# The split weight tiles of gate and up, moved from 224 to 64 bytes off the 2 KB raster

## The reference

```python
def swiglu(h, w_gate, w_up, w_down):
    return (jax.nn.silu(h @ w_gate) * (h @ w_up)) @ w_down

h = rms_norm(x, g_ffn1_pre)
x = x + 0.5 * rms_norm(swiglu(h, w_ffn1_gate, w_ffn1_up, w_ffn1_down), g_ffn1_post)
h = rms_norm(x, g_mix_pre)
# token mixing: one projection of h, stick-breaking attention (8 heads x 64),
# retention (4 heads x 128), two gated branches, one output projection
x = x + rms_norm(merged @ w_out, g_mix_post)
h = rms_norm(x, g_ffn2_pre)
x = x + 0.5 * rms_norm(swiglu(h, w_ffn2_gate, w_ffn2_up, w_ffn2_down), g_ffn2_post)
```

## Time and profile before

| | us |
|---|---|
| median of 3 runs | 1366.22 |
| lowest and highest | 1366.1 and 1368.4 |
| the profiled execution | 1366.35 |
| its span | 1364.3 |
| TensorE busy | 1349.2 |
| VectorE busy | 1029.3 |
| ScalarE busy | 734.3 |

### The profile page before, as it was taken

How to read it: one execution, slowest core, us unless ns; L and a number is a source line. 1 busy time by engine, 2 the same in 40 slices (tenths; PEclk the granted TensorE clock), 3 DMA queues, 4 the chain that set the end, 5 groups by cost and what they waited for, 6 DMA issues and landing times.

```text
span 1364.3 us, 22732 instructions
## 1 busy us (share of the span) xinstructions
PE 1349.2 (99%) x8668; PEld 1209.1 (89%) x8668; DVE 1029.3 (75%) x1124; ACT 734.3 (54%) x1008; POOL 99.9 (7%) x156
## 2 busy tenths in 40 slices
PE   8999999999999999999999999999999999999998
PEld 7999999999888888777778888799999999988886
DVE  7987888788988964667664334689788878888896
ACT  6554554555765743666653233555454455458663
POOL 0000000001330000322210000000000000025000
PEclk9999999999999999999999999999999999999999
DMA  6333332347994555212113345333333234399844
GB/s 209 109 92 109 123 108 82 117 123 248 197 202 155 191 179 139 77 48 63 47 47 93 93 122 189 106 100 113 113 123 108 80 120 123 112 284 198 177 139 154
DMA packets 152935, 177.71 MB, mean 130 GB/s; under 512 B 5552, under 2 KB 116400, under 8 KB 152752
## 3 DMA queue, kind: packets, MB, share of 16 engines
q1 hardware_dynamic: 139536, 151.54, 35.2%
q0 software_dynamic: 13056, 25.17, 10.2%
q10 hardware_dynamic: 288, 0.26, 0.1%
HBM read 170.66 MB, written 6.29 MB: 130 GB/s over the span
## 4 chain that ended last, share of the span: by engine, by line
PE 91%; DVE 4%; ACT 2%; DMA 1%; issue 1%; POOL 0%; SPq 0%; DVEq 0%; ACTq 0%; POOLq 0%
PE ps L797 14%; PE ps L800 14%; PE ps L799 14%; PE ps L898 8%; PE ps L899 7%; PE ps L900 7%; PE ps L730 6%; PE ps L732 5%; PE ps L731 5%; PE ps L737 2%; PE ps L738 2%; PE ps L739 2%; PE ps L1090 1%; DMA w_raw<-w_ffn_up 1%; PE ps L1045 1%
## 5 line engine op out<-in xcount | busy, mean ns | idle before, releaser
L797 PE MATMUL ps<-s_hi,u_hi 128*128 128x256 f32 x960 | 268.0, 279 | 1.5 <-DVE u_lo L1805 0.8
L800 PE MATMUL ps<-s_hi,u_lo 128*128 128x256 f32 x960 | 267.7, 279 | 0.0
L799 PE MATMUL ps<-s_lo,u_hi 128*128 128x256 f32 x960 | 267.7, 279 | 0.0
L797 PE MATMUL ps<-a_hi,u_hi 128*128 128x256 f32 x808 | 225.7, 279 | 1.1 <-DVE a_lo L1760 1.1
L800 PE MATMUL ps<-a_hi,u_lo 128*128 128x256 f32 x808 | 225.4, 279 | 0.0
L799 PE MATMUL ps<-a_lo,u_hi 128*128 128x256 f32 x808 | 225.3, 279 | 0.0
L1291 ACT ACTIVATE u_hi<-w_sum 128x1024 fp32r<-128x1024 f32 x120 | 124.0, 1057 | 173.0 <-DVE w_sum L1834 80.3
L797 PEld LDWEIGHTS ps<-s_hi,u_hi 128*128 128x128 f32 x960 | 180.5, 188 | 2.1 <-ACT m_c L1325 1.1
L799 PEld LDWEIGHTS ps<-s_lo,u_hi 128*128 128x128 f32 x960 | 180.5, 188 | 0.0
L800 PEld LDWEIGHTS ps<-s_hi,u_lo 128*128 128x128 f32 x960 | 180.5, 188 | 0.0
L898 PE MATMUL ps<-w_hi,l_hi 128*128 128x512 f32 x448 | 174.9, 390 | 0.1
(11 more groups left out here) (222 smaller groups left out, 2529.1 us busy)
## 6 DMA issues: line engine op xcount, KB each, us to landing
w_raw<-w_ffn_gate SPq DMA_DIRECT2D x64, 512.0 KB, 5.2
w_raw<-w_ffn_up SPq DMA_DIRECT2D x64, 512.0 KB, 4.7
d_sum<-w_ffn_down POOLq DMA_DIRECT2D x48, 512.0 KB, 12.3
w_raw<-w_in SPq DMA_DIRECT2D x44, 512.0 KB, 4.2
w_raw<-w_ffn_down SPq DMA_DIRECT2D x40, 512.0 KB, 4.2
d_sum<-w_ffn_down SPq DMA_DIRECT2D x16, 512.0 KB, 8.0
x_tok<-x SPq DMA_DIRECT2D x8, 512.0 KB, 6.0
d_m_raw<-w_ffn_down SPq DMA_DIRECT2D x8, 512.0 KB, 8.4
```

Of the source, the lines that this page charges most:

```text
L797: pe.matmul(o, wh, hi[:, k, :], start=first and f == 0 and k == 0, stop=False, skip_group_check=True)
L799: pe.matmul(o, wh, lo[:, k, :], start=False, stop=False, skip_group_check=True)
L800: mm = pe.matmul(o, wl, hi[:, k, :], start=False, stop=last and k == KH - 1, skip_group_check=True)
```

## The change

One constant is changed. It moves the start of `u_hi`, `u_lo` and `w_sum` in all seven slots.

```diff
 LINE = 2048
 GAP = 512
-UP_OFF = 224
+UP_OFF = 64
```

## The result

The kernel after takes 1361.26 us, median of 14 runs, against 1366.34 of before; the ratio is 0.9927 with an interval of 0.991 to 0.9945. It is faster, where 1384 was forecast, and inside the range given (1348 to 1387). The single runs say more than the median. Before: eight between 1365.8 and 1366.4 us, six between 1368.4 and 1368.9. After: five at 1351, seven at 1361 and two at 1371 us, and nothing between.

What follows compares the result with a forecast made beforehand. The prediction took TensorE's matmul start-to-start distance to bound the kernel. 1366.3 us plus 17.7 us (3.33 ns on 5304 matmuls with u) gave 1384.0 us, range 1348 to 1387.

Steps and rivals of the forecast that it cites:

- TensorE alone bounds the loops; an edit of its distance is paid in full.: Gate-and-up loops of both FFNs: time is the number of matmuls times the start-to-start distance, 116.7 ns, with TensorE never waiting.
- VectorE, ScalarE and the queues cost nothing.: Subtractions and copies into the moved tiles: offsets 0 and 224 within 2 ns, priced at nothing; no DMA changed.
- The distance with u at 224 is 116.7, with b22 on the grid 120.0, and the place of the stationary tile is the difference.: Gate-and-up matmuls: 3.3 ns longer with the stationary tile on the streamed tile's 512-byte grid than 224 off it.
- The rule of the Trainium skill: Weight loads on TensorE: separate read ports, so no offset matters and the time is 1366 us; basis of the no-change rival, 0.28.
- Two rows cannot decide it; I take the nearer one and price the new offset at 120.0 ns.: Matmuls with u: offset 64 priced like offset 0, 3.33 ns more on each of 5304; chance 0.34.
- a supposed grid of 64: Weight loads of u: if reads conflict on any 64-byte grid, offset 64 is exactly as bad as 0.
- the sum's 17.7 us of loss: Matmuls with u in gate and up: 3.33 ns times 5304, all on the path.
- The faster case: Second rival, loads of u behind lines 797 to 800: shorter step becomes steady, 17.7 us gained, 1348.6 us; chance 0.24.
- the short step is never kept: Argument against the faster rival: at 224 the steady mean is the same in loop and straight code.
- One offset, one distance: Matmuls with u: the forecast gave offset 64 a single unknown distance, priced at 120.0 ns.
- all three rivals: No change, 1366 us (0.28); faster, 1348.6 us (0.24); part of the loss, 1375 us (0.14 with other amounts).

Runs made afterwards that it cites:

- off_0: Kernel before with all u tiles at offset 0 instead of 224: 1382.28 us, ratio 1.0111.
- base_64: Kernel before with all large tiles, streamed and stationary, 64 bytes higher and u at offset 0 from the raster: 1382.48 us in one run.
- the survey: Two runs of the kernel before with a different offset for each of the seven u slots, multiples of 32 from 0 to 416 bytes: 1375.71 and 1375.55 us.
- after_again: The kernel after, unchanged, run seven more times: 1350.95, 1351.34, four from 1360.86 to 1361.03, and 1371.57 us.

## Why the prediction was wrong

- *TensorE alone bounds the loops; an edit of its distance is paid in full.* Right. Busy time and span moved by the same 15 us.
- *VectorE, ScalarE and the queues cost nothing.* Right: 1 and 3 ns on the two rows.
- *The distance with u at 224 is 116.7, with b22 on the grid 120.0, and the place of the stationary tile is the difference.* Right, and shown: off_0 makes the loops run at 120.0, base_64 shows that it is u's place against the other large tiles (that the streamed one is meant is argued). The rule of the Trainium skill weighed there, from "TensorE: Matmul & The Clock Gate", "Step-by-step: what each phase is for" (a read port each, and no bandwidth taken), would have u's place cost nothing; the runs disagree, with 113.3 to 120.0 ns for it.
- *"Two rows cannot decide it; I take the nearer one and price the new offset at 120.0 ns."* This is the step that failed: the price of the new offset was taken from b22's, by nearness in bytes and by a supposed grid of 64. Offset 64 has 113.3 or 117.8 ns in every trace, and never 120.0. The distance does not follow nearness to 0 (the survey has 160 at 119.7, 192 at 117.7 and 224 at 116.8), and there is no grid of 64 bytes. In place of the sum's 17.7 us of loss there was a gain of 15.2 us in the profiled run.
- *The rival that was right.* The faster case gave its mechanism (the shorter step becomes the steady one), its place (the loads of u behind lines 797 to 800), its mark (under 116 ns) and its price: 3.3 ns on 5304 matmuls, 1348.6 us. Measured 113.3 ns and 1351.17. Most of the missing 2.5 us are the stretches at 117.8 ns ahead of 64.2 us and up to 928.7 us, where the longer distance still held: some 520 matmuls x 4.5 ns = 2.3 us. The reason it gave, reads that pass each other on a grid, is shown by no run. The argument against it, "the short step is never kept", took the absence in one offset's trace for a bar on all.
- *One offset, one distance.* This was taken for granted in the sum and in all three rivals, and is wrong at 64 and 192: two steady distances, 113.3 and 117.8 ns, one below and one above the 116.7 of 224. Hence three groups of times. The median of 1361 us, 5 us below before, is one loop at each distance; no case of the prediction had it. That it lies inside the range given is owed to the range's width over losses and gains, not to the mechanism.
- The groups of before, 1366.2 and 1368.6 us, and one run of before at 1371.16 in the series of after_again, are likely of this kind also. They are some 2.4 us apart, and a loop at 117.8 ns for 116.7 would cost 1.1 ns x 2300 = 2.5 us. The trace of before, whose loops have 116.7, has the longer distance in the first group of its second FFN, 36 distances in 4.24 us:

```profile
889.30 0.28 PE L797 MATMUL ps<-a_hi,u_hi 128*128 128x256 f32 x1
...
893.54 0.28 PE L797 MATMUL ps<-a_hi,u_hi 128*128 128x256 f32 x1
```

  No trace of a 1368 run was taken, so this is argued only.

## What to carry to other kernels

When TensorE is busy all the time and each matmul has its own weight load, the place of the stationary tile against the streamed one is a tuning knob worth a per cent: read the distance from start to start, not the group's mean, and survey several offsets in one run by giving each buffer its own. Such a survey shows that the place counts, but does not rank the offsets: here it had 224 quickest and 64 at 117.9 ns, while alone, or mixed with 192, 64 can hold 113.3. So run each candidate by itself, several times. Look at single runs before a median: groups of equal times some us apart mean a rhythm that a stretch falls into, and a change of offset inside the loop can hold the stream in the better one. An offset found for 256 streamed columns has to be looked for anew at 512.

## What the runs showed of the hardware

- With 256 streamed fp32r columns and a 128-column load for each matmul, the distance is 113.3 to 120.0 ns, by the offset of the stationary tile; offsets 256 bytes apart (0, 32, 64, 96, 128 and 160 were compared) give the same within 0.3 ns. With 512 columns it is 226.7 to 234 ns.
- At offsets 64 and 192 two steady distances exist at the same clock of 1.00. The distance changed behind a matmul that came 0.06 us late (after), another 0.02 us late (after_again), and idle times of 0.35 and 0.47 us, but not behind one 0.04 us late; a distance once taken lasted for some 2300 matmuls.
- Changing between the offsets 64 and 192 (or 224) every few products led back to 113.3 ns by the next group at the latest, in the three traces taken.
- What in the reads makes it so was not found: no trace shows where or whether the two reads meet, and no offset between the multiples of 32 was tried.
